# Attention of a hybrid decoder step: prompt-head turns and sample-sequence turns of one layer joined into one loop

## What is computed

```python
def fox_prompt(q, k, v, logf):          # causal over 272 tokens
    s = einsum('bqgrd,bkgd->bgrqk', qi, kp) * ATTN_SCALE
    s = s + c_query[..., None] - c_key  # c = cumsum of log forget values
    s = where(kpos <= qpos, s, -inf)
    return einsum('bgrqk,bkgd->bqgrd', softmax(s), vp)

def fox_sample(cache_k, cache_v, cache_logf, page_table, layer, q, k, v, logf):
    kp = cache_k[layer][page_table]     # 8 pages of 128 positions for each sequence
    vp = cache_v[layer][page_table]
    lfp = cache_logf[layer][page_table]
    r = cumsum(lfp, reverse=True) - lfp # bias of every past position
    s_past = q.kp * ATTN_SCALE + r_key + cn
    s_self = where(tril, q.k * ATTN_SCALE + cn_query - cn_key, -inf)
    p = softmax(concat([s_past, s_self]))
    return p[..., :past] @ vp + p[..., past:] @ v
```

## Time and profile before

| | us |
|---|---|
| median of three runs | 1519.92 (1519.23 to 1521.69) |
| the profiled execution | 1520.04 |
| its span, first to last instruction | 1518.3 |
| TensorE busy in the span | 1324.1 (87%) |
| VectorE, ScalarE, GpSimd busy | 490.4, 244.0, 206.5 |
| attention, first transfer issue to last copy | 487.1 to 724.6 |

### The profile page before, as it was taken

One profiled execution on the slowest core, in us unless ns is written; L12 is line 12 of the kernel. 1 busy time (PEld: TensorE's weight loads), 2 busy tenths in 40 slices (PEclk: granted clock), 3 DMA queues, 4 the chain that ended last, 5 costly groups with the idle time before them and its releaser, 6 DMA issues. The chain is left out here.

```text
span 1518.3 us, 19514 instructions
## 1 busy us (share of the span) xinstructions
PE 1324.1 (87%) x6133; PEld 792.5 (52%) x6133; DVE 490.4 (32%) x1080; ACT 244.0 (16%) x644; POOL 206.5 (14%) x401
## 2 busy tenths in 40 slices
PE   5899999999995898877899999669999989899990
PEld 3666667666763455554566664444444443434440
DVE  2236564555456474333000001342122121211123
ACT  1132233223322343222000000000000000000001
POOL 3033442244224111010000000000000000000003
PEclk9799999899997898999899999689999999999995
DMA  6033324332422227553965360259999999999974
GB/s 194 19 111 104 96 83 142 102 98 83 142 59 57 47 50 259 180 149 92 253 139 137 87 217 0 109 232 427 428 430 428 428 428 429 428 429 428 429 303 128
DMA packets 171554, 318.30 MB, mean 210 GB/s; under 512 B 21147, under 2 KB 148563, under 8 KB 159235
## 3 DMA queue, kind: packets, MB, share of 16 engines
q1 hardware_dynamic: 162610, 302.03, 55.0%
q10 hardware_dynamic: 6864, 8.94, 1.7%
q0 software_dynamic: 2048, 6.95, 1.7%
HBM read 289.20 MB, written 28.68 MB: 209 GB/s over the span
## 5 line engine op out<-in xcount | busy, mean ns | idle before, releaser
L670 PE MATMUL psg<-stretch 128*128 128x336 f32 x512 | 159.4, 476 | 11.3 <-DVE h_sample_out L648 9.6
L1734 PE MATMUL ph<-w_gate_up,x_gathered 128*64 128x512 f32 x704 | 162.4, 612 | 0.6 <-DVE x_gathered L1673 0.6
L670 PEld LDWEIGHTS psg<-stretch 128*128 128x128 f32 x512 | 103.6, 204 | 69.0 <-DVE h_sample_out L648 15.4
L1751 PE MATMUL py<-w_down,h_t 128*64 128x512 f32 x512 | 118.5, 605 | 22.8 <-DMA w_down<-in_w_exp_down 22.8
L1685 DVE SCALAR_TENSOR_TENSOR h_gate<-h_tanh,ph 128x256 f32<-128x256 f32 x32 | 13.5, 421 | 344.7 <-ACT h_tanh L1642 344.7
L1734 PEld LDWEIGHTS ph<-w_gate_up,x_gathered 128*64 128x64 f32 x704 | 52.0, 135 | 105.8 <-issue 105.8
L1709 PE MATMUL px<-chunk_rows,yT 128*128 128x192 f32 x516 | 97.9, 332 | 0.0
L1709 PEld LDWEIGHTS px<-chunk_rows,yT 128*128 128x128 f32 x516 | 82.6, 190 | 27.3 <-issue 27.3
L585 DVE SCALAR_TENSOR_TENSOR x_conv<-x_padded,conv_wh,x_conv 128x360 f32<-128x360 f32 x96 | 57.0, 594 | 100.5 <-ACT x_conv L534 89.6
L679 PE MATMUL psg<-stretch 128*128 128x256 f32 (+1 forms) x384 | 84.5, 380 | 0.0
L1347 PE MATMUL psm<-stretch,w_merge 128*128 128x336 f32 x256 | 76.0, 456 | 7.0 <-DMA w_merge<-in_w_in 7.0
(11 more groups left out here) (413 smaller groups left out, 1755.8 us busy)
## 6 DMA issues: line engine op xcount, KB each, us to landing
w_down<-in_w_exp_down SPq DMA_DIRECT2D x32, 2048.0 KB, 25.8
w_gate_up<-in_w_exp_gate SPq DMA_DIRECT2D x22, 2048.0 KB, 22.7
w_gate_up<-in_w_exp_up SPq DMA_DIRECT2D x22, 2048.0 KB, 27.4
stretch<-in_w_exp_gate SPq DMA_DIRECT2D x10, 2048.0 KB, 23.4
stretch<-in_w_exp_up SPq DMA_DIRECT2D x10, 2048.0 KB, 28.0
stretch<-in_w_in SPq DMA_DIRECT2D x16, 1024.0 KB, 5.3
stretch<-in_w_in SPq DMA_DIRECT2D x16, 512.0 KB, 7.6
h<-in_state_ssm SPq DMA_DIRECT2D x16, 512.0 KB, 4.8
```

The lines of the kernel that those rows point to most:

```text
L670: mm = pe.matmul(ps[m][:, 0:T], wg[:, k, P * m:P * m + P], S["xnT"][:, k, :], start=(k == 0), stop=(k == KT - 1))
L1734: mm = pe.matmul(ph[64 * j:64 * j + 64, :], xg[u // 3][:, k, BLK * (u % 3):BLK * (u % 3) + BLK], w_gu[w][:, :, k, :].rearrange("p g (f t) ...
L1751: mm = pe.matmul(py[h][64 * j:64 * j + 64, :], ht[:, k % 2, k // 2, :], w_dn[h][:, k, 512 * j:512 * j + 512], start=(k == 0), stop=(k == 3))
```

## The change

Attention is written anew; its arithmetic is the same. The order is now:

- The first half of q's weights (2 MB) is loaded to w_group by SyncE within the state-space phase, behind its last channels. The second half is one 2 MB load at the head of SyncE's stream in attention. All eight q projections stand first in TensorE's stream, six of them ahead of the past bias, the seventh behind it and the eighth behind the first pair's scores.
- The past bias takes 15 products: GpSimd adds up the log-forget pages (lsum) for the part with ones. GpSimd then sends each sequence's 16 rows of it, every row eight times, to a tile of 128 rows (rrep), and VectorE adds it to the scores in the instruction that takes the maximum (tensor_tensor_reduce). The selector product, the masks and the copies of L923 to L927 go.
- Turn i holds the prompt pair i and sequence i, unrolled. The keys are transposed in four chunks, two ahead of the pair's products and two behind the probabilities' transposes; ScalarE and VectorE each copy one chunk of two.
- Keys and values have semaphores of their own; values are asked for only before their product. Values of sequence 1 are loaded behind the eighth projection, into the buffer of the late weights, which also holds pr and pts.
- The 16 tail rows of the heads are stacked: 8 heads x 16 rows in one tile of 128, scored, normalised and multiplied twice (u = 0, 1) in the last turn.
- The blank rows are written by GpSimd at the head of the state-space phase from a tile of their own. The setup's semaphores are cleared and freed after it, and the tile self01 and its fill in the setup go.

The diff, cut to its core:

```diff
@@ -169,13 +169,6 @@
             pool.memset(S["mask_t"][:, 256:320], NEG)
             keep(S["mask_t"][:, 320:336], [[-1, 16]], 0, 1, fill=NEG)
 
-            pool.memset(S["self01"][:, :, :], 1.0)
-            pool.drain()
-            m4 = S["self01"][:, :, :].rearrange("k s (h q) -> k s h q", q=8)
-            keep(m4, [[8, 8], [0, 16], [1, 8]], 0, -1)
-            pool.drain()
-            keep(m4, [[-8, 8], [0, 16], [0, 8]], 0, 1)
-            pool.drain()
...
         pool_passed = S["pool_passed"]
-        zero_ok = sem("zero_ok")
+        zero_ok, blank_ok, blank_out = sem("zero_ok"), sem("blank_ok"), sem("blank_out")
+        blank = tsb("blank", [P, D])
...
+        nc.clear_and_free_semaphores(S["setup_sems"])
         block = ctx.enter_context(nc.Block())
...
                 send_h(g - 1)
+            sp.wait_ge(f_ps, 4 * G)
+            sp.dma_start(S["w_group"][:, :, 0:512], A["w_in"].rearrange("a (t p) c -> p (a t) c", p=P)[
+                :, :, C_Q:C_Q + 512]).then_inc(S["wq_in"], 16)
             send_h(G - 1)
             sp.wait_ge(cv_ev, 2)
...
+            sp.wait_ge(blank_out, 16)
...
             pool.memset(yss[:, :], 1.0).then_inc(zero_ok, 1)
+            pool.memset(blank[:, :], 0.0).then_inc(blank_ok, 1)
+            pool.wait_ge(blank_ok, 1)
+            pool.dma_start(S["ydram"][LEAST_BLK * BLK:SLOTS, :].rearrange("(b p) d -> p b d", p=P),
+                           bc(blank[:, :].unsqueeze(1), [P, (NBLK - LEAST_BLK) * BLK // P, D])).then_inc(blank_out, 16)
             with pool.Fori(0, G) as g:
...
         @block.sync
         def _(sp):
+            sp.dma_start(wq[1], win[:, :, C_Q + 512:C_Q + 1024]).then_inc(late_in, 16)
             sp.dma_start(ptab[:, :], A["page_table"].rearrange("(a s) b -> a (s b)", a=1)).then_inc(tab_in, 16)
             sp.wait_ge(tab_in, 16)
...
             with sp.Fori(0, NSEQ) as s:
                 for b in range(NPG):
                     pg = sp.value_load(ptab[0:1, bass.ds(s * NPG + b, 1)], min_val=0, max_val=POOL - 1)
                     sp.dma_start(lfp[:, b, bass.ds(s, 1), :], cl[:, bass.ds(pg, 1), :]).then_inc(lf_in, 16)
-            for half in range(2):
-                load_kv(half, half, False)
-            sp.wait_ge(kx_ok, 1)
-            sp.dma_start(S["ydram"][LEAST_BLK * BLK:SLOTS, :].rearrange("(b p) d -> p b d", p=P),
-                         bc(blank.unsqueeze(1), [P, (NBLK - LEAST_BLK) * BLK // P, D])).then_inc(blank_out, 16)
...
+            first = pages_of(0)
+            load_k(first, 0)
...
+            second = pages_of(1)
+            load_k(second, 1)
+            sp.wait_ge(q_ps, 8)
+            load_v(second, 1)
             with sp.Fori(1, NSEQ // 2) as i:
                 for half in range(2):
-                    load_kv(2 * i + half, half, True)
-            sp.wait_ge(blank_out, 16)
+                    s = 2 * i + half
+                    pages = pages_of(s)
+                    sp.wait_ge(kt_ps, 4 * s - 4)
+                    load_k(pages, half)
+                    sp.wait_ge(so_ps, s - 1)
+                    load_v(pages, half)
 
...
+            pool.wait_ge(lf_in, 16 * NSEQ * NPG)
+            pool.sem_inc(gate)
+            pool.tensor_copy(lsum[:, NPG - 2, :, :], lfp[:, NPG - 1, :, :])
+            for b in range(NPG - 3, -1, -1):
+                pool.drain()
+                i = pool.tensor_tensor(lsum[:, b, :, :], lsum[:, b + 1, :, :], lfp[:, b + 1, :, :], ALU.add)
+            i.then_inc(ls_ok, 1)
+
+            for s in range(NSEQ):
+                pool.wait_ge(r_ev, 2)
+                if s >= 2:
+                    pool.wait_ge(m_ok, s - 1)
+                pool.dma_start(rrep[:, s % 2, :],
+                               bc(rall[16 * s:16 * s + 16, :].unsqueeze(1), [16, 8, PAST])).then_inc(rr_in[s % 2], 16)
...
+            for t in range(6):
+                q_out(t)
+            act.wait_ge(r_ps, 1)
...
+            q_out(6)
+            q_out(7)
+            probs(0, 0)
+            probs(0, 1)
+            keys_out(0, 0)
+            keys_out(0, 1)
+            for i in range(NSEQ):
+                pt_out(i)
+                act.wait_ge(m_ok, i + 1)
+                act.activation(pr, pr, ACT.Exp, bias=nb[:, 0:1], accum_out=sm[:, 0:1]).then_inc(e_ok, 1)
+                act.activation(pself[:, i, 8 * i:8 * i + 8], sself[:, :], ACT.Exp, bias=nb[:, 0:1],
+                               accum_out=sm[:, 1:2]).then_inc(e_ok, 1)
+                if i < NSEQ - 1:
+                    keys_out(i + 1, 0)
+                else:
...
+                act.wait_ge(o_ps, i + 1)
+                act.activation(S["oT"][:, i, 0:256], o_acc, ACT.Copy).then_inc(o_ev, 1)
+                act.wait_ge(pp_ps, 3 * i + 1)
+                act.activation(pts[:, 0:4, :], seqb[:, 0, :].rearrange("p (b c) -> p b c", c=P),
+                               ACT.Copy).then_inc(pp_eva, 1)
...
+                if i < NSEQ - 1:
+                    probs(i + 1, 0)
+                    keys_out(i + 1, 1)
+                    probs(i + 1, 1)
...
+            def pair_max(t):
...
+                    for c, (c0, n, m0) in enumerate(((0, 128, 128), (128, 256, 0))):
+                        k = 2 * g2 + c
+                        v.tensor_tensor_reduce(sc[:, g2, c0:c0 + n], pair[g2][:, c0:c0 + n],
+                                               S["mask_d"][:, m0:m0 + n], 1.0, -3.0e38, ALU.add, ALU.max,
+                                               mxp[:, k:k + 1])
...
+                    cq = S["c_q"][:, 0:2, head(t, g2)]
+                    v.tensor_tensor(mxp[:, 2 * g2:2 * g2 + 2], mxp[:, 2 * g2:2 * g2 + 2], cq, ALU.add)
+                    v.drain()
+                    v.tensor_tensor(nm[:, 2 * g2:2 * g2 + 2], cq, mxp[:, 2 * g2:2 * g2 + 2],
+                                    ALU.subtract).then_inc(nm_ok, 1)
...
+            def seq_max(s):
+                v.wait_ge(ss_ps, s + 1)
+                v.wait_ge(rr_in[s % 2], 16 * (s // 2) + 16)
+                v.tensor_tensor_reduce(sself[:, :], own_ps, selfb[:, s, :], 1.0, -3.0e38, ALU.add, ALU.max, mx[:, 0:1])
+                v.tensor_tensor_reduce(pr, seqb[:, :, :].rearrange("p a c -> p (a c)"), rrep[:, s % 2, :], 1.0,
+                                       -3.0e38, ALU.add, ALU.max, mx[:, 1:2])
+                v.drain()
...
+                v.scalar_tensor_tensor(nb[:, :], ncnq[:, s:s + 1], -1.0, mx[:, 2:3], ALU.mult,
+                                       ALU.subtract).then_inc(m_ok, 1)
+
...
+            spread_q(0)
+            v.wait_ge(r_ps, 2)
+            v.tensor_copy(rall[:, 512:1024], seqb[:, 1, :]).then_inc(r_ev, 1)
+            pair_max(0)
...
+            keys_out(0, 0)
+            pair_norm(0)
+            keys_out(0, 1)
+            for i in range(NSEQ):
+                if i:
+                    pair_norm(i)
+                seq_max(i)
+                if i:
+                    rows_out(i - 1)
+                if i < NSEQ - 1:
+                    keys_out(i + 1, 0)
+                    pair_max(i + 1)
+                else:
...
+                v.wait_ge(pp_ps, 3 * i + 2)
+                v.tensor_copy(pts[:, 4:8, :], seqb[:, 1, :].rearrange("p (b c) -> p b c", c=P))
+                v.wait_ge(pp_ps, 3 * i + 3)
+                v.tensor_copy(ptself[:, :], ownt_ps).then_inc(pp_evv, 1)
+                if i < NSEQ - 1:
+                    keys_out(i + 1, 1)
+                v.wait_ge(e_ok, 2 * i + 2)
...
+                v.wait_ge(so_ps, i + 1)
+                v.tensor_scalar(oe[:, :], so_acc, sm[:, 3:4], None, ALU.mult).then_inc(so_ev, 1)
+            rows_out(NSEQ - 1)
...
+            def outputs(t):
...
                 pe.wait_ge(pt_ev, 2 * t + 2)
-                pe.wait_ge(o_ev, t + 1)
-                for c, r in enumerate(ROWS):
+                pe.wait_ge(sot_ev, t)
...
+            def turn_keys(s, chunks):
+                half = s % 2
+                for c in chunks:
+                    n = 4 * s + c
+                    if c == 0:
+                        pe.wait_ge(k_in[half], 128 * (s // 2) + 128)
+                        if s == 0:
+                            pe.wait_ge(q_ev, 16)
+                    if n >= 2:
+                        pe.wait_ge(kt_eva if c % 2 else kt_evv, n // 2)
...
-                for b in range(2):
-                    pe.matmul(psc[:, b, :], scur[:, :], rall[:, 512 * b:512 * b + 512], start=True, stop=False)
-                pe.wait_ge(kt_ev, 2 * s + 2)
-                pe.wait_ge(kt_evb, 2 * s + 2)
...
+                pe.wait_ge(kt_evv, 2 * s + 2)
+                pe.wait_ge(kt_eva, 2 * s + 2)
                 for b in range(2):
                     for a in range(2):
-                        q_ = slice(64 * a, 64 * a + 64)
-                        mm = pe.matmul(psc[q_, b, :], qcur[:, a, q_], kts[:, a, 512 * b:512 * b + 512],
-                                       start=False, stop=True)
+                        mm = pe.matmul(seqb[q_rows(a), b, :], qblk[:, s, a, :], kts[:, a, 512 * b:512 * b + 512],
```

(67 more changed lines are left out.)

515 lines of the change are left out of this document (240 added, 275 removed).

## The result

The changed kernel takes 1524.2 us (median of 18 runs, 1520.18 to 1531.66) against 1518.97 for the kernel before in the same number of runs (1513.56 to 1522.58): ratio 1.004, 95% interval 1.0026 to 1.0053. It is slower by 0.4%; 1503 was forecast, with 1491 to 1514 as the range, so the measured time lies above it. The profiled execution took 1520.78, its span is 1519.0.

What follows compares the result with a forecast made beforehand. The sample half of attention was taken to be paced by SyncE at 13.7 us a sequence. Attention ending 17.0 us earlier and 0.5 for a barrier: 1520.04 - 17.0 + 0.5 = 1503.5, given as 1503, range 1491 to 1514.

Steps and rivals of the forecast that it cites:

- Step 1 and 2: Start of attention: six projections first; page table waits 8.2 us behind 2 MB load, first log-forget page at 496.0, all 576.0.
- The hole: TensorE stands still some 55 us after its sixth projection, from 520.6, until the log-forget pages have landed and been summed.
- Rivals A and D: Log-forget pages: A, they land while projections run, 1444, chance 3%; D, page table doesn't wait behind 2 MB, 1498, 13%.
- Step 3 and 4: Past bias, last projections: GpSimd's sums 3.7 us, projection 7 done at 596.5, first sequence scores 6.9 us later, 603.4.
- Step 5 (turn): Attention turn's own length: 12.4 us, first 10.7, last 14.4; fused add and maximum taken as 1.23 us.
- rival B: Fused add-and-maximum instruction in attention runs far slower than the plain maximum; at three times, 1532; chance 8%.
- Step 6 (SyncE's pace): SyncE's part unchanged: V(2) at 614.1, 64.35 us to K(7) at 678.4, attention ends at 707.6, gain 17.0 us.
- Step 7 (small things): Outside attention: blank rows moved to GpSimd, removed fill, setup semaphores; nearly all hidden, 0.5 us taken for a second barrier.
- Rival C: GpSimd is stuck handing out the 8 MB of blank rows, up to 23.5 us; 10 to 12 lost, 1515; chance 8%.
- Rival E: Turns go by their own chain at 14 us or more, from late copies or hand-overs; 1508 to 1512; chance 13%.

Runs made afterwards that it cites:

- the fastest kernel: Changed kernel with log-forget loads in the SSD stage, r_rows transfers read from a memory copy, half the values pages issued by GpSimd: 1425.68 us, ratio 0.9403.

## Why the prediction was wrong

- **Step 1 and 2 (order, table behind the 2 MB)** right: the first page goes out 0.5 us early. The 2 MB load itself landed after 8.9 us (8.2 was taken, 6.8 by the estimate beside it). The hole is 61.3 us; the forecast speaks of some 55, but its own times, 520.6 to 579.7, make 59. Moving the loads away gave back 57.1 us of time, and 62.7 from the first load of attention to the first sequence scores. Rivals A and D are out.
- **Step 3 and 4 (bias, projections)** right: 601.56 against 603.4. GpSimd's seven sums took 575.12 to 578.98, 3.9 us (3.7).
- **Step 5 (turn)** right in the first turn, 10.6 us (601.56 to 612.18) against 10.7. The fused instruction, which no row before showed, took what was assumed for it:

```profile
L1101 DVE CUSTOM_DVE_ANT_0 q_weights_late<-pa_seq,r_rows x8: 1219/1221/1221, 603.7 to 717.7; 128x1024 f32<-128x1024 f32 x8
```

  1.22 us (min, median and max in ns) beside 1.23; rival B, slower, is out. The later turns were sized at 12.4 and take 11.5 by their own chain (704.09 to 715.59 here, 11.49 in the fastest kernel), 0.9 too long, which cost the sum nothing that shows: from K(7) to the start of the last turn it took 14.9 us, 14.8 forecast. The last turn took 12.4 instead of 14.4.
- **Step 6 (SyncE's pace) is the step that failed.** It said that SyncE's part is unchanged and took the 64.35 us from V(2) to K(7) from the old trace, and it had SyncE wait for the first sequence's output ahead of V(2). SyncE's instructions are indeed the same, but eight transfers of 512 KB were added beside them, and the step gave those no row and no price, since they are issued by another engine. V(2) went out at 622.71 instead of 614.1 (+8.6): the output was there at about 612.2, but SyncE came late, since the eight reads ahead of K(2) took 8.9 us (a transfer is issued at 606.03) and K(2) itself 7.68 (another at 616.66). V(2) to K(7) took 78.01 (+13.7), with four transfers issued in between. That makes 22.3 us. Behind K(7) it went 1.9 us faster than forecast, so attention ends 20.4 late. With six transfers away the same stretch takes 64.06 and the kernel 1500.71 (one run), so the rest of the sum was right to about 3 us.
- **Step 7 (small things)** right as a sum: the page table goes out at 487.24 (487.7), and from the last copy of attention to the end the kernel takes 1520.78 - 727.98 = 792.8 us, where 1503.5 - 707.6 = 795.9 was reckoned, 3.1 less. So 1503.5 + 20.4 - 3.1 is the 1520.8 of the profiled execution. Rival C is out: GpSimd issued the 8 MB in 1.41 us and went on, though they took 24.7 us to land, and the stage ahead of attention isn't longer.
- Rival E had the right side of things, turns of 14 us or more, but by another cause. No rival held a transfer against another engine's transfers, so of the 10% for a slower kernel 8 went to an instruction that was harmless.

The trace of before has no transfer that reads 16 neighbouring rows, so its 7.1 us could not be read there. But the diff shows 4 MB of new traffic in a stage that SyncE's pages pace, and that was a term with unknown price, to be bounded from both sides. How an issue on SyncE comes to stand still while those packets are moved, no run shows; only that it does, in register reads and issues alike, and by how much.

## What to carry over

Where a transfer queue is the pace of a stage, what a change adds to any other queue may lie on the path: price it first, by where it reads. Here a broadcast out of 16 neighbouring on-chip rows was dear, and a small product, or a source in memory, was cheaper. And loads whose addresses are known long ahead can go into an earlier stage's waits, where 78 us of issues cost nothing that could be seen.

## What the runs showed of the hardware

- The transfers' packets (means, nearly all of the bytes in rows of 4 KB) take 0.48 us read from 16 neighbouring on-chip rows eight times, 0.255 when the 16 rows lie 8 apart, 0.17 from 128 rows once, 0.20 from memory. From ScalarE's queue it is the same as from GpSimd's (26.6% of 16 x 102 us for 918 packets, 0.47).
- The harm to SyncE's issues isn't set by the packet's time alone: per transfer it is 3.5 us, 1.5 and 0.9 for these three on-chip sources, and none that can be seen for the source in memory with its 0.20 us, read once or eight times. Each is one trace.
- After 9 to 10 us of idleness TensorE's next eight transposes took 1.97 us instead of 1.04, at a granted clock of 0.50. Whether that cost time here, where SyncE was the pace, no run tells.
